# Token-major residual and 512-column matmuls in a three-block transformer kernel: what changes in time

## The reference

```
mod = c_act @ ada_w + ada_b                 # shift, scale, gate of each part
h = rms_norm(x, g) * (1 + scale) + shift
moba:  x = x + gate * (merged @ w_out)
conv:  u = causal_dwconv(h @ w_up, conv_w, conv_b); u_g, u_v = split(u)
       x = x + gate * ((silu(u_g) * u_v) @ w_down)
plain: g, u = split(h @ w13)                # 1024 x 5632, hidden 2816
       x = x + 0.5 * gate * ((silu(g) * u) @ w2)
swa, fox: x = x + gate * (mixer(h, w_in) @ w_out)
```

## Time and profile before

| | |
|---|---|
| median of three runs | 1680.42 us |
| profiled execution: its own time | 1680.4 us |
| profiled execution: its span | 1680.4 us |
| TensorE busy | 1589.1 us, 95% |
| VectorE busy | 1148.2 us, 68% |
| ScalarE busy | 644.9 us, 38% |
| moved by DMA | 335.70 MB, 200 GB/s |

### The profile page before, as it was taken

How to read it: one execution, slowest core, us unless ns; L and a number is a source line. 1 busy time by engine, 2 the same in 40 slices (tenths; PEclk the granted TensorE clock), 3 DMA queues, 4 the chain that set the end, 5 groups by cost and what they waited for, 6 DMA issues and landing times.

```text
span 1680.4 us, 29943 instructions
## 1 busy us (share of the span) xinstructions
PE 1589.1 (95%) x12172; PEld 1518.8 (90%) x12177; DVE 1148.2 (68%) x1868; ACT 644.9 (38%) x793; POOL 10.0 (1%) x19
## 2 busy tenths in 40 slices
PE   5599999999989999999989999999999999989998
PEld 4588998999989999886679999899998987889998
DVE  4873876988888676863467767786677576664544
ACT  1343334544453333433334333433334345343332
POOL 1000000000000000000000000000000000000000
PEclk8697999999999999995599999999999999799999
DMA  7963765877648667551167676487665553445552
GB/s 229 297 204 125 247 205 178 277 251 245 223 136 306 238 230 249 173 171 51 51 201 266 231 250 228 151 281 249 236 231 174 181 201 101 151 151 187 187 175 75
DMA packets 281979, 335.70 MB, mean 200 GB/s; under 512 B 5490, under 2 KB 264206, under 8 KB 281780
## 3 DMA queue, kind: packets, MB, share of 16 engines
q1 hardware_dynamic: 279888, 328.30, 58.5%
q0 software_dynamic: 1440, 6.18, 1.2%
q10 hardware_dynamic: 580, 0.23, 0.1%
HBM read 333.58 MB, written 1.10 MB: 199 GB/s over the span
## 4 chain that ended last, share of the span: by engine, by line
PE 88%; DVE 7%; DMA 2%; issue 1%; ACT 1%; SPq 0%; DVEq 0%; ACTq 0%
PE bank L1110 25%; PE bank L1111 24%; PE bank L1112 24%; PE bank L1183 4%; DVE ada_sum L703 2%; PE bank L1310 2%; PE bank L1208 2%; DMA ada<-in_ada_w 2%; PE bank L1296 2%; PE bank L1202 1%; PE bank L1288 1%; PE bank L1287 1%; DVE lo L686 1%; PE bank L1276 1%; PE bank L1264 1%
## 5 line engine op out<-in xcount | busy, mean ns | idle before, releaser
L1110 PE MATMUL bank<-h_hi,hi 128*128 128x256 f32 x2256 | 652.8, 289 | 35.5 <-DVE h_lo L763 31.6
L1111 PE MATMUL bank<-h_lo,hi 128*128 128x256 f32 x2256 | 646.6, 287 | 0.0
L1112 PE MATMUL bank<-h_hi,lo 128*128 128x256 f32 x2256 | 646.3, 286 | 0.0
L420 ACT ACTIVATE hi<-raw 128x2048 fp32r<-128x2048 f32 x215 | 411.3, 1913 | 578.4 <-PE bank L1112 531.3
L686 DVE TENSOR_TENSOR lo<-raw,hi 128x2048 fp32r<-128x2048 f32 x215 | 491.8, 2289 | 177.8 <-ACT hi L420 176.1
L1110 PEld LDWEIGHTS bank<-h_hi,hi 128*128 128x128 f32 x2256 | 441.7, 196 | 39.9 <-issue 38.2
L1111 PEld LDWEIGHTS bank<-h_lo,hi 128*128 128x128 f32 x2256 | 441.9, 196 | 0.0
L1112 PEld LDWEIGHTS bank<-h_hi,lo 128*128 128x128 f32 x2256 | 441.4, 196 | 0.0
L1110 PE MATMUL bank<-o_hi,hi 128*128 128x256 f32 x1072 | 309.3, 289 | 0.9 <-DVE o_lo L885 0.9
L1112 PE MATMUL bank<-o_hi,lo 128*128 128x256 f32 x1072 | 305.0, 285 | 0.0
L1111 PE MATMUL bank<-o_lo,hi 128*128 128x256 f32 x1072 | 305.0, 285 | 0.0
(11 more groups left out here) (172 smaller groups left out, 1186.4 us busy)
## 6 DMA issues: line engine op xcount, KB each, us to landing
raw<-in_ffn_w SPq DMA_DIRECT2D x132, 1024.0 KB, 5.2
ada<-in_ada_w SPq DMA_DIRECT2D x94, 1024.0 KB, 5.1
raw<-in_w_up SPq DMA_DIRECT2D x22, 1024.0 KB, 5.1
raw<-in_w_in SPq DMA_DIRECT2D x16, 1024.0 KB, 6.5
raw<-in_fox_w_in SPq DMA_DIRECT2D x12, 1024.0 KB, 5.3
raw<-in_w_down SPq DMA_DIRECT2D x11, 1024.0 KB, 5.4
raw<-in_swa_w_in SPq DMA_DIRECT2D x6, 1024.0 KB, 5.4
raw<-in_w_out SPq DMA_DIRECT2D x4, 1024.0 KB, 5.1
```

The costliest lines, as they stand in the source:

```text
L420: nc.scalar.activation(hi[:, split_of(w), :], raw[:, raw_of(w), :], ACT.Copy).then_inc(hi_ready, 1)
L1110: mm(outp, wh, xh, start=start, stop=False, skip_group_check=True)
L1111: mm(outp, wh, xl, start=False, stop=False, skip_group_check=True)
L1112: return mm(outp, wl, xh, start=False, stop=stop, skip_group_check=True)
```

## The change

1. *The residual is token-major*: `x` is two tiles of 128 tokens by 1024 features. Out, down and plain up products hold 128 tokens (a 128 x 128 piece of h, hidden or attention output) and move 512 weight columns. 7440 matmuls of 256 columns become 3720 of 512; 2880 of 256 columns stay (input projections, branch units, conv's up units). The out weights are loaded as rows (2 tiles of k by 1024 columns).
2. *Plain up units* hold 256 gate columns beside the same 256 value columns, for four tiles of k; two such units (k halves) make a group. Each is loaded with two DMAs of 512 KB. Silu and product are token-major; four transposes (`turn_hidden`) turn the hidden tile.
3. *Norm per token tile*: ScalarE squares with a running sum, VectorE adds, ScalarE takes the root, VectorE the reciprocal, ScalarE scales; TensorE transposes (`turn_x`); VectorE applies scale and shift, ScalarE rounds, VectorE subtracts, per tile of 128 x 128. The gate is spread to rows by eight matmuls (`gate_rows`) and copied by ScalarE; the residual is a product and an addition per 512 columns. The matmuls with ones and with zeros, and the transposes at the end, are gone.
4. *Five shared slots*: `raw` and `lo` lie in the same memory (lo overwrites raw), `NS = 5`. A load now waits until TensorE has done the unit five before.
5. *Modulation on VectorE alone*: chunks of 512 columns, in four pieces of 512 KB (two operations of 512 columns each), two slots; TensorE sums with four one-column matmuls. The units multiplied by TensorE are gone. Tables say after which unit, step or group how many pieces are loaded and used (`PIECES_GROUP = [3, 3, 3, 3, 2, 2, 2, 2, 2, 2, 0]` in feed-forward stages).
6. The loops are written out.

```diff
-        raw = sb("raw", [P, NBUF, UNIT])
-        hi = sb("hi", [P, NBUF, UNIT], F32R)
-        lo = sb("lo", [P, NBUF, UNIT], F32R)
-        ada = sb("ada", [P, 2, KD, CW])
-        ada_sum = sb("ada_sum", [P, 2, CW])
-        xT = sb("xT", [P, KD, T])
+        hi = sb("hi", [P, NS, UNIT], F32R)
+        lo_base = nc.sbuf_base
+        lo = sb("lo", [P, NS, UNIT], F32R)
+        raw = nc.alloc_sbuf_tensor_at("raw", [P, NS, UNIT], F32, offset=lo_base)
+        ada = sb("ada", [P, 2, 2, 512])
+        ada_sum = sb("ada_sum", [P, 2, 512])
+        x = sb("x", [P, 2, D])
...
 # SyncE
+            def free_slot(w):
+                if w >= NS:
+                    sp.wait_ge(unit_done, w - NS + 1)
...
+                free_slot(w)
+                for g in range(2):
+                    first = FF * g + CW * j
+                    sp.dma_start(raw_of(w, 4)[:, :, CW * g:CW * (g + 1)],
+                                 all_rows(up)[:, 4 * part:4 * part + 4, first:first + CW]).then_inc(raw_full[w % NS], 16)
...
+            def load_pieces(count):
...
+                    if n >= 2:
+                        sp.wait_ge(ada_step, 2 * (n - 2) + 8 * PRO_CHUNKS + 2)
+                    sp.dma_start(ada[:, n % 2, :, :], ada_columns(c)[:, 2 * q:2 * q + 2, :]).then_inc(ada_full[n % 2], 16)
...
+                    for j in range(FIT):
+                        count = PIECES_GROUP[j - 1] if j and chunks_in(s) else 0
+                        load_up(s, j, 0)
+                        load_pieces(min(count, 2))
+                        load_up(s, j, 1)
+                        load_pieces(max(count - 2, 0))
+                        if j:
+                            load_down(s, j - 1)
+                    load_down(s, FIT - 1)
...
 # VectorE, conv
                 taps(0)
-                split_lo(n + 2, i)
+                if j:
+                    split_to(order_of(s, j - 1, 2))
                 taps(2)
...
+                    split_to(order_of(s, j + 1, 0))
+                    pieces(PIECES_GROUP[j])
+                    columns(COLS_GROUP.get(j, 0))
+                    split_to(order_of(s, j + 1, 1))
...
 # VectorE, plain
+                if j:
+                    split_to(order_of(s, j - 1, 2))
...
+                mul(s, j, 0)
+                mul(s, j, 1)
+                if j < FIT - 1:
+                    split_to(order_of(s, j + 1, 0 if j else 1))
+                    dve.wait_ge(hid_hi_done, hid_count(s, j, 0))
+                    nc.vector.tensor_tensor(hid_lo[:, j % 2, :, :].rearrange("p a b -> p (a b)"), S[:, :],
+                                            hid_hi[:, j % 2, :, :].rearrange("p a b -> p (a b)").bitcast(F32),
+                                            ALU.subtract).then_inc(hid_ready, 1)
+                    split_to(order_of(s, j + 1, 1))
+                    if some:
+                        pieces(PIECES_GROUP[j])
...
 # TensorE
+            def rows_times(w, tiles, xh, xl, t, k0, first, last, s):
+                for h in range(2):
+                    for k in range(tiles):
...
+                        mm(outp, xk_hi, wh[:, k, cut], start=start, stop=False, skip_group_check=True)
+                        mm(outp, xk_hi, wl[:, k, cut], start=False, stop=False, skip_group_check=True)
+                        ins = mm(outp, xk_lo, wh[:, k, cut], start=False, stop=stop, skip_group_check=True)
...
+                    else:
+                        pe.wait_ge(mul_done, 2 * (FIT * f + j) - 1)
+                        up(s, j, 0, 0)
+                        pe.wait_ge(mul_done, 2 * (FIT * f + j))
+                        up(s, j, 0, 1).then_inc(unit_done, 1)
...
+                        up(s, j, 1, 0).then_inc(gu_done, 1)
+                        up(s, j, 1, 1).then_inc(unit_done, 1)
...
+                    if 0 < j < last:
+                        down(s, j - 1, 0)
+                        turn_hidden(s, j, 0)
+                        turn_hidden(s, j, 1).then_inc(hid_turned, 1)
+                        down(s, j - 1, 1).then_inc(unit_done, 1)
```

More of the change, by code:

```diff
@@ L57 @@
 V_UNITS = {"moba": [4, 5], "swa": [1], "fox": [8, 9, 10, 11]}
[L58 removed]
+V0 = [sum(len(V_UNITS.get(k, [])) for k in KINDS[:s]) for s in range(NST)]
 OUT_UNITS = {"moba": 20, "swa": 6, "fox": 12}
[L61 to L68 removed]
@@ L979, in _ @@
                                     ALU.mult).then_inc(cols_done, 1)
-            ada_sum_of(2, 0)
+            for i in range(3, 6):
+                pro_piece(i)
+            columns(2)
             for n in range(2):
```

1041 lines of the change are left out of this document (539 added, 502 removed).

## The result

The changed kernel took 1785.28 us (median of four runs, 1782.66 to 1789.33) beside 1679.37 for the kernel before: ratio 1.063, 95% interval 1.0605 to 1.0654. That is 106 us slower. The forecast was 1720 with a range of 1655 to 1775: the direction was right, the size and the range were not.

The account below looks back on a forecast made before the run. It took waits on TensorE's product lines (73% of the span) as the bound. Stage terms moba 263, conv 247, plain 220, 436 and 191, swa 160, fox 198, end 5 summed to 1720 us; range 1655 to 1775.

Parts of the forecast that it names:

- the attention part's sentence on moba: Moba attention: twelve quarters of 0.9 to 1.8 us leave TensorE, eight pieces of 1.5 reach VectorE; -8 us taken.
- Products: Plain, down and out products: 3720 of 512 columns at 0.216 us each; 89 us less where TensorE alone decides.
- Rival (4): Products of 512 columns so short, about 131 ns, that VectorE bounds the plain groups; about 1555 us; chance 0.01.
- The third piece: Plain stages: down load waits behind third modulation piece; TensorE stalls 7.9 us, then three times 3.5 to 4.4; 19.4 a stage.
- Conv: Conv stage: VectorE's lo order and third pieces make TensorE wait, up to 2.1 and 3.7 us; 247 us from 204.9.
- Boundary: Start of conv and attention stages: first product 14 us after the last, instead of 8.3; nothing covers the gap.
- swa: Swa attention stage: a step falls from 5.67 to 4.0 us, VectorE taking a piece a step; 160 us from 181.9.
- fox: Fox attention stage: no gain from moving pieces to VectorE, 6 us added for a half clock; 198 us from 192.8.
- Rival (2): The clock falls in fox and moba attention, +17 and +8 us, 1745 us in all; chance 0.13.
- (1): Products of 512 columns take 0.240 us each, +62 us, 1782 us in all; chance 0.12.
- (3): Third piece and down load land before needed, so stalls vanish: 1616 us, or partly, 1616 to 1674; chance 0.20.
- (5): Whole kernel: stalls and savings cancel, 1680 us; chance 0.06.

Follow-up runs that it names:

- e12: The change alone, but in moba TensorE takes six sums one unit later and the gate rows behind units 11 and 12: 1754.38 us, ratio 1.0457.
- e1: The change, but in moba SyncE issues the modulation pieces before the unit load beside them, not behind it: 1778.41 us, ratio 1.0578.
- e9: The change alone, but in moba only the first two of 32 modulation pieces are loaded, the others computed from the same slots: 1771.88 us, ratio 1.0542.
- e2: The change, but in feed-forward stages SyncE issues the third modulation piece behind the down load, not ahead of it: 1749.22 us, ratio 1.0414.
- e14: Change with GpSimd-issued pieces, e6's conv order, e7's boundaries, e12's sum places, no pieces in a feed-forward stage's first group, three in groups 1 to 6: 1660.26 us.
- e5: On top of e2, in conv VectorE forms lo of the next value unit before the modulation pieces, not behind them: 1736.8 us, ratio 1.0324.
- e6: On top of e2, in conv ScalarE and VectorE work one unit further ahead, as in the kernel before: 1721.39 us, ratio 1.0236.
- e7: The change alone, but at conv and attention boundaries both token tiles' residual, squares, root and scaling precede the eight steps of either: 1787.23 us, ratio 1.0627.
- e3: The change, but each matmul of 512 columns issued as two of 256 with the same held piece: 1819.16 us, ratio 1.0833.

## Why the prediction was wrong, step by step

*The step that failed is the attention part's sentence on moba*: "twelve quarters of 0.9 to 1.8 us go from TensorE, and eight pieces of 1.5 come to VectorE: between 0 and -12, I take -8". It took eight pieces and the quarters as the only difference, counted work by engine and never followed the chain of a sum, though the prediction did exactly that for the plain group and conv. A sum on TensorE needs four pieces, VectorE takes them behind lo of a unit, and a unit load on SyncE now waits for TensorE (`unit_done`, not `lo_ready`): a ring. Moba came out 48 us over the forecast, three quarters of the error. e12 shows that the places of the sums close the ring: 35 of the 48. e1 and e9 show that the queue (12) and queue and transfers together (18) lengthen it. The other 13 us are open; waits of 10.4, 6.4, 4.7, 3.5 and 2.4 us still stand in e12.

*Products*: the term was mis-sized. 0.227 measured, 0.216 taken; the bf16 row was not a measure of this format, whose spacing is 13.3 ns above its columns and not 2. On the last plain stage, where TensorE alone decides, 792 x 0.0107 is 8.5 us, and the stage came out 5.9 over the forecast. The plain stages with pieces have the same term, and came out 6.5 to 8.1 each over the forecast. Rival (4), with its far shorter products, is refuted by the same 0.227.

*The third piece*: right in mechanism and place, and near in size (15.8, 16.1 and 18.2 us of waits in the three stages for a forecast of 19.4), and e2 confirms it for the plain stages. Two points were not in it: 4.5 of the 7.3 us in the first group stayed in e2 and went only with the pieces of that group (e14); and in conv, where I gave the third piece a part of the blame, e2 changed nothing.

*Conv*: 242.4 for 247. VectorE's order was named as the cause and it is (e5, e6: 13 and 25 us). The waits before value units are 3.2 to 3.8 us for a forecast of 3.7, those before gate units 2.0, or 1.1 with a sum, for 2.1 and 1.2. The total is luck in part: a wait of 6.5 before group 1's gate unit wasn't foreseen (32.3 us up to there, where the sum had 27.7), and from group 5 on the stage took 118.3 us for 125.3.

*Boundary*: 13.0 to 14.5 us for a forecast of 14. That a shorter gap pays little wasn't foreseen: in conv and swa the full clock came back no earlier (e7).

*swa* 161.1 for 160, and by the way that was named: most steps take 3.2 to 3.9 us where the sum had 4.0, after 5.67 before. *fox* 190.5 for 198. Most of the 6 us for a half clock in fox didn't come: the granted clock of the stage was 0.89 after 0.92. Rival (2) didn't happen.

*Rivals*: (1) gave 1782, close to the result, but for a reason that the trace refutes: 0.240 would have been needed. (3), the cheap landing, is refuted by the waits in the trace, most of which e2 took away by the order of the loads alone. (5), that stalls and savings cancel, didn't happen. The range ended at 1775, short of (1)'s 1782 by choice, and no case in it had moba's waits.

## What to carry to other kernels

When a kernel moves small sums between engines, follow each sum from its load to its reader in every stage, not only in the ones with the most work. A consumer that stands one unit too early on the engine that everything else waits for closes a ring with the loads which that engine releases; here moving six sums, and one group of gate rows, one unit later was worth 31 us, about as much as all the longer matmuls (34, e3). And work moved off a path at no cost on paper (pieces on an engine with room) has to be placed behind what others wait for: VectorE waiting for a load in the middle of its list holds all that is behind it.
